# Behind the experts: joins ahead of the roots, roots in pairs, a scale that moves into the turn

## Chip, cores, metric

One core of a Trainium2 chip runs the whole network in one launch. The metric is the device time in microseconds (us). Before the change three runs gave 2161.83, 2163.40 and 2168.58 us, median 2163.4. TensorE (PE) multiplies, VectorE (DVE), ScalarE (ACT) and GpSimd (POOL) work on rows, SyncE (SP) issues the weight loads. The granted clock of TensorE has two levels, 1.2 and 2.4 GHz, shown as 0.50 and 1.00.

## What is computed

Two layers of a mixer with attention and a routed mixture of 32 experts (first block), then a dilated attention and a state-space layer (second block). The model is 1024 wide, 256 tokens in two tiles of 128, and 256 context tokens in two further tiles for layer 0. Two places of it matter here:

```
# end of layer 0: the experts' two rows per token are added, weighted; then layer 1 begins
x = x + w0 * y0 + w1 * y1
h = modulate(rmsnorm(x, norm_mix_g[1]), shift, scale)     # 4 tiles: latent and context
q, k, v = h @ odd_w_in[0]

# end of layer 1: the same sum, the final norm, and the second block's first norm
x = rmsnorm(x + w0 * y0 + w1 * y1, final_g)
h = rms_norm(x, attn_pre_norm_2[0])
h = dilated_attention_mixer(h, attn_w_in_2[0], ...)
```

## The kernel before

Each engine runs its own program, written out by hand; they meet at semaphores. `ev(name)` raises one when an instruction ends, `at(name)` is the value to wait for, `dm(name)` is raised by a DMA. `vstep` lets VectorE wait for its own last instruction. `XS[:, t, :]` holds the rows of tile t, `HT` the turned (transposed) activations, `ST` small columns of statistics, `AR` a large workspace cut by hand, `RG` the ring of weight slots, `PS[0..7]` the PSUM banks.

**Behind the experts of layer 0** (odd_begin). `act_combine` (L1934 to L1937) has ScalarE's queue load the experts' rows, one load of 1 MB for each of four tiles, `z_load0..3`. `dve_join` (L1929 to L1932) adds them to XS in two passes. ScalarE squares and sums the tile (L2005). Then the root: `dve_rstd` (L486) writes the mean (L491), ScalarE takes the square root (`act_root`, L508), VectorE inverts it and refines it with one Newton step (L493 to L501, with n=1 three tensor_scalar, with n>1 the forms with two tensors). The identity scaled by the result is `DG` (L2032), and TensorE multiplies each 128x128 block of XS by it (L1995), which scales and turns at once. ScalarE copies six of the eight blocks out of PSUM with scale and shift from `COLS` (L2017), VectorE two (L2043). `COLS` of layer 1 come from `pe_odd_cols`, `dve_odd_raw` and `dve_odd_cols` (L473, L413, L420, L423), which TensorE and VectorE do on the way. Both engines' loops are staggered over six steps: step i joins tile i, takes the root of tile i-1, copies out tile i-2. Banks alternate between tiles, so tile t waits for the copies of tile t-2.

Then `pe_odd` projects (L2074 for the first weights). In between it turns the bias of the attention (L2110), 7 heads at a time. `act_odd` loads what that needs from ScalarE's queue: it waits until tile 3 is turned, issues three table loads (L2115, L2117) and then the bias loads (L2096). SP issues the weights of layer 1 (L3134) once `z_load3` has landed (L3116).

**Behind the experts of layer 1** (final, L2324 to L2358). Two tiles. VectorE joins both, multiplying each by final_g (`gained`, L2341); ScalarE squares the rows before and after that (L2325, L2328). Then, tile after tile on VectorE: the root of the final norm, its square into the sum of the gained rows (L2346, L2348), the root of the next norm, the product of both (L2350), and the rows multiplied by that and by attn_pre_norm_2, `PG1` (L2351, into `W1[t]`). `pe_turn` transposes W1[t] against the plain identity (L533), ScalarE copies the halves into HT (L539), and L2501 is the first projection of the dilated attention. The scaled rows themselves go back into XS (L2354). POOL has no part; its next work is the masks (L2660), behind `mask_load` and `finished`. ScalarE's exponential and sine (L2362 to L2368) and VectorE's tables (L2384 on) run beside the first projections.

Of the kernel before, what the change touches and what calls it, by code (L numbers as in the profile page):

```python
# [155 lines left out]
def build(nc, I, K, out, stop=None, dump=None):  # L156
    ctx = ExitStack()
    with ctx:
# [1821 lines left out]
        DG = [ar(0, 128), ar(KK, 128)]  # L1980
# [5 lines left out]
        def pe_odd_begin(pe):  # L1986
            pe_odd_cols(pe)
            for t in range(4):
# [4 lines left out]
                for k in range(8):  # L1993
                    bank, c = odd_bank_of(t, k)
                    m = pe.matmul(bank[:, c:c + 128], XS[:, t, 128 * k:128 * k + 128], DG[t % 2], start=True, stop=True,  # L1995
                                  skip_group_check=True)
                    if k in (5, 7):
                        m.then_inc(*ev("turned", "mix1", t, k // 7))

        def act_odd_begin(act):  # L2000
            act.dma_start(AB[:, 4:12], I["ada_b_pad"][1][:, 4:12]).then_inc(*dm("ab2_load"))
            for i in range(6):
                if i < 4:
                    act.wait_ge(*at("joined_rows", i))
                    act.activation(E0.Z[i][:, 0, :], XS[:, i, :], ACT.Square,  # L2005
                                   accum_out=ST[:, i:i + 1]).then_inc(*ev("squares", ("mix1", i)))
                if 1 <= i <= 4:
                    t = i - 1
                    act_root(act, ("mix1", t), at_=t)
                if i >= 2:  # L2010
                    t = i - 2
                    if t == 0:
                        act.wait_ge(*at("ada_cols", 1, 3))
                    act.wait_ge(*at("turned", "mix1", t, 0))
                    for k in range(6):
                        bank, c = odd_bank_of(t, k)
                        ins = act.activation(HT[:, k, 128 * t:128 * t + 128], bank[:, c:c + 128],  # L2017
                                             ACT.Identity, scale=COLS[1][:, 1, t // 2, k:k + 1],
                                             bias=COLS[1][:, 0, t // 2, k:k + 1])
                    ins.then_inc(*ev("turned_out", "mix1", t, 0))  # L2020

        def dve_odd_begin(v):
            for i in range(6):
                if i < 4:
                    v.wait_ge(*at(f"z_load{i}", 0))
                    dve_join(v, E0, i, ev("joined_rows", i))
                if 1 <= i <= 4:
                    t = i - 1
                    dve_rstd(v, ("mix1", t), D, at_=t)
                    if t >= 2:  # L2030
                        v.wait_ge(*at("turned", "mix1", t - 2, 1))
                    v.tensor_scalar(DG[t % 2], IDN[:], ST[:, 16 + t:17 + t], None, MUL).then_inc(*ev("diagonal", t))  # L2032
                if i == 1:
                    dve_odd_raw(v, 1)
                if i == 2:
                    dve_odd_cols(v)
                    v.wait_ge(*at("ada_cols", 1, 3))
                if i >= 2:
                    t = i - 2
                    v.wait_ge(*at("turned", "mix1", t, 1))  # L2040
                    for k in range(6, 8):
                        bank, c = odd_bank_of(t, k)
                        ins = v.tensor_scalar(HT[:, k, 128 * t:128 * t + 128], bank[:, c:c + 128],  # L2043
                                              COLS[1][:, 1, t // 2, k:k + 1], COLS[1][:, 0, t // 2, k:k + 1], MUL, ADD)
                    ins.then_inc(*ev("turned_dve", "mix1", t, 1))
# [275 lines left out]

        def act_final(act):
            for t in range(2):
# [6 lines left out]
                act_root(act, ("final", t), at_=t)  # L2330
                act_root(act, ("dil", t), at_=2 + t)
# [906 lines left out]
```

## Time and profile before

| | |
|---|---|
| median of 3 runs | 2163.4 us |
| profiled execution, its own time | 2162.5 us |
| its span | 2160.7 us |
| PE busy | 1963.8 us (91%) |
| DVE busy | 657.7 us (30%) |
| ACT busy | 371.1 us (17%) |
| POOL busy | 321.8 us (15%) |
| DMA, mean | 269 GB/s |

In a timeline a row is: start, time covered, engine, line, operation, out<-in, how many instructions were merged; in brackets the idle time of the engine before them and what ended it. A suffix q is the engine's queue, here the issue of DMAs; PEld loads weights. Two records stand for one matmul in float32. A transpose has one record.

### The profile page before, as it was taken

How to read it: one execution, taken by the hardware profiler on the slowest of the kernel's cores; microseconds unless marked ns; L12 is line 12 of the kernel's file. 1: busy time of each engine (PE TensorE's matmuls, PEld its weight loads, DVE VectorE, ACT ScalarE, POOL GpSimd, SP SyncE). 2: the span in 40 equal slices, each digit the busy share in tenths (PEclk: the TensorE clock that was granted, in tenths of full speed). 3: DMA queues.
4: the chain of work that ended last, by engine and by line, in shares of the span. 5: the costliest groups of instructions: out<-in, count | busy, mean ns of one | idle time of the engine just before them, and what ended most of it. 6: DMA issues, size and time to landing. Idle time of an engine off the chain costs nothing.

```text
span 2160.7 us, 33840 instructions
## 1 busy us (share of the span) xinstructions
PE 1963.8 (91%) x14657; PEld 1221.4 (57%) x14657; DVE 657.7 (30%) x1544; ACT 371.1 (17%) x825; POOL 321.8 (15%) x264
## 2 busy tenths in 40 slices
PE   5999999999999859999999989988859999997998
PEld 3565565555555445546555444444346676674884
DVE  1334373212222232115331111111145031145752
ACT  3133410000000020113310000000021220132131
POOL 0125411000000000114310000000020060040120
PEclk9999999999999979999999999999979999998999
DMA  9352399999999985217399999999764314417221
GB/s 366 130 199 97 120 381 408 426 427 427 426 425 426 425 325 157 84 43 274 129 381 426 427 423 427 426 421 426 334 243 156 140 57 156 143 53 195 79 90 59
DMA packets 129617, 581.14 MB, mean 269 GB/s; under 512 B 19178, under 2 KB 30602, under 8 KB 104752
## 3 DMA queue, kind: packets, MB, share of 16 engines
q1 hardware_dynamic: 103856, 545.28, 63.3%
q10 hardware_dynamic: 19488, 27.16, 3.7%
q0 software_dynamic: 6112, 6.39, 0.8%
q8 instruction: 121, 1.98, 0.4%
q14 instruction: 40, 0.33, 0.0%
HBM read 569.21 MB, written 21.38 MB: 273 GB/s over the span
## 4 chain that ended last, share of the span: by engine, by line
PE 68%; DMA 19%; DVE 6%; issue 3%; ACT 2%; POOL 2%; ACTq 1%; SPq 0%; POOLq 0%; DVEq 0%
DMA RG<-in_moe_w 16%; PE banks L1524 13%; PE banks L2501 8%; PE banks L1549 6%; PE banks L1500 4%; PE banks L2503 4%; PE banks L1076 4%; PE banks L2074 3%; PE banks L667 3%; PE banks L2076 3%; PE banks L2702 3%; PE banks L2899 2%; PE banks L797 2%; PE banks L341 2%; PE banks L825 2%
## 5 line engine op out<-in xcount | busy, mean ns | idle before, releaser
L1524 PE MATMUL banks<-RG,HT 128*64 128x256 f32 x3616 | 429.1, 391 | 31.9 <-DMA RG<-in_moe_w 29.8
L1524 PEld LDWEIGHTS banks<-RG,HT 128*64 128x64 f32 x3616 | 252.3, 135 | 215.1 <-DMA RG<-in_moe_w 48.3
L1754 POOL DMA_INDIRECT y_rows<-AR x64 | 64.0, 1000 | 871.1 <-DVE AR L1563 870.5
L1533 DVE TENSOR_TENSOR AR<-AR,banks 128x256 f32<-128x256 f32 x64 | 38.6, 603 | 481.4 <-ACT AR L1529 430.3
L1549 PE MATMUL banks<-RG,AR 128*64 128x512 f32 x752 | 171.7, 598 | 3.6 <-DVE AR L1542 3.1
L2501 PE MATMUL banks<-HT,RG 128*128 128x256 f32 x768 | 170.2, 383 | 0.7 <-ACT HT L539 0.7
L2501 PEld LDWEIGHTS banks<-HT,RG 128*128 128x128 f32 x768 | 147.0, 192 | 23.4 <-issue 2.4
L1529 ACT ACTIVATE AR<-banks 128x256 f32<-128x256 f32 x64 | 24.5, 383 | 747.2 <-PE banks L1524 747.2
L1500 PE MATMUL banks<-AR 128*128 128x256 bf16 (+1 forms) x1152 | 149.4, 277 | 2.0 <-DVE AR L1488 1.5
L1500 PEld LDWEIGHTS banks<-AR 128*128 128x128 bf16 x1152 | 108.5, 98 | 33.6 <-issue 18.3
L1549 PEld LDWEIGHTS banks<-RG,AR 128*64 128x64 f32 x752 | 50.0, 136 | 94.2 <-issue 83.4
L2074 PE MATMUL banks<-HT,RG 128*128 128x256 f32 (+1 forms) x256 | 87.4, 500 | 3.8 <-ACT HT L2017 1.8
L2503 PE MATMUL banks<-RG,HT 128*128 128x512 f32 x192 | 84.1, 594 | 0.0
L1076 PE MATMUL banks<-RG,HT 128*128 128x512 f32 x192 | 83.3, 594 | 0.8 <-DVE HT L887 0.8
L341 PE MATMUL banks<-RG,SC 128*32 128x128 f32 x1536 | 55.5, 306 | 28.9 <-DMA RG<-in_ada_w 18.2
L904 POOL TENSOR_SCALAR AR<-AR,ST 128x768 f32<-128x768 f32 (+1 forms) x24 | 45.0, 1883 | 245.6 <-DVE ST L882 245.2
L904 POOL TENSOR_SCALAR AR<-AR,SVT 128x512 f32<-128x512 f32 x27 | 42.0, 1563 | 216.8 <-DVE SVT L882 216.7
L2074 PEld LDWEIGHTS banks<-HT,RG 128*128 128x128 f32 x256 | 49.4, 196 | 42.0 <-issue 36.3
L667 PE MATMUL banks<-RG,HT 128*128 128x512 f32 (+1 forms) x192 | 69.0, 521 | 1.7 <-DVE HT L647 1.7
L341 PEld LDWEIGHTS banks<-RG,SC 128*32 128x32 f32 x1536 | 48.5, 124 | 35.5 <-issue 29.1
L1513 ACT ACTIVATE HT<-banks 128x256 f32<-128x256 f32 x128 | 49.0, 383 | 104.7 <-PE banks L1500 104.7
L1549 PE MATMUL banks<-AR 128*64 128x512 f32 x272 | 62.1, 598 | 1.0 <-DVE AR L1542 1.0
(473 smaller groups left out, 2402.4 us busy)
## 6 DMA issues: line engine op xcount, KB each, us to landing
RG<-in_moe_w SPq DMA_DIRECT2D x160, 2048.0 KB, 24.1
AR<-in_moe_w SPq DMA_DIRECT2D x32, 2048.0 KB, 12.2
RG<-in_ada_w SPq DMA_DIRECT2D x24, 2048.0 KB, 8.4
RG<-in_attn_w_in SPq DMA_DIRECT2D x20, 2048.0 KB, 7.6
RG<-in_odd_w_in SPq DMA_DIRECT2D x6, 2048.0 KB, 25.7
RG<-in_ssm_w_in SPq DMA_DIRECT2D x4, 2048.0 KB, 9.5
AR<-y_rows ACTq DMA_DIRECT2D x6, 1024.0 KB, 7.0
RG<-in_even_w_in SPq DMA_DIRECT2D x2, 2048.0 KB
```

Source lines behind the costliest of these rows:

```text
L341: m = pe.matmul(q[32 * j:32 * j + 32, :], SC[:, k, :], w[:, k, 128 * j:128 * j + 128], start=k == 0, stop=k == 7, skip_group_check=True)
L667: m = pe.matmul(PS[b][:, 0:wd], HT[:, k, 128 * t:128 * t + 128], w[:, k, :], start=k == 0, stop=k == 7)
L904: g.tensor_scalar(u["pb"][x], u["pb"][x], A.small_of(s, 3)[:, x:x + 1], None, MUL).then_inc(*ev("weighed_pool", name, s, x))
L1076: m = pe.matmul(PS[b], HT[:, k, 128 * t:128 * t + 128], w[:, k, :], start=k == 0, stop=k == 7)
L1500: m = pe.matmul(p, E.HB[t][:, i, k, :], E.one_hot(g, t), start=t == 0 and i == 0, stop=t == E.nt - 1 and i == 2)
L1524: m = pe.matmul(p[64 * h:64 * h + 64, 256 * i:256 * i + 256], x[:, k, :], w[:, h, k], start=k == 0, stop=k == 7, skip_group_check=True)
L1549: m = pe.matmul(q[64 * h:64 * h + 64, :], x, w2[:, i, 512 * h:512 * h + 512], start=i == 0, stop=i == 3)
L2074: m = pe.matmul(p[:, 0:wd], w[:, k, 128 * j:128 * j + 128], HT[:, k, 0:wd], start=k == 0, stop=k == 7)
L2076: m = pe.matmul(p, HT[:, k, 128 * j:128 * j + 128], w[:, k, :], start=k == 0, stop=k == 7)
L2501: m = pe.matmul(p[:, 0:256], w[:, k, 128 * j:128 * j + 128], HT[:, k, 0:256], start=k == 0, stop=k == 7)
L2503: m = pe.matmul(p, HT[:, k, 128 * j:128 * j + 128], w[:, k, :], start=k == 0, stop=k == 7)
L2702: m = pe.matmul(PS[2 * h + t], src[:, k, 128 * t:128 * t + 128], w[:, k, :], start=k == 0, stop=k == 7)
```

## The change

In the first place all four joins stand ahead of the later work: VectorE joins tiles 0, 1 and 2 (with the modulation steps of layer 1 between), takes the root of tile 0, joins tile 3, takes the root of tile 1, and then the roots of tiles 2 and 3 in one pass of two columns. Copies out of PSUM come behind all that. There are four diagonals instead of two, so none waits for another's use. Of tiles 2 and 3 VectorE copies four blocks out, ScalarE four. A one-element square root ahead of ScalarE's first square loads the table of roots.

In the second place the roots of both tiles are taken together, again with an early one-element root. W1[t] is the gained row times PG1, without the scale; VectorE makes W1[0], POOL makes W1[1]. The scale goes into two diagonals, `DG2`, and TensorE multiplies by them instead of transposing.

```diff
-        DG = [ar(0, 128), ar(KK, 128)]
+        DG = [ar(128 * t, 128) for t in range(4)]
+
+        def odd_on_act(t):
+            return 6 if t < 2 else 4
...
-                    m = pe.matmul(bank[:, c:c + 128], XS[:, t, 128 * k:128 * k + 128], DG[t % 2], start=True, stop=True,
+                    m = pe.matmul(bank[:, c:c + 128], XS[:, t, 128 * k:128 * k + 128], DG[t], start=True, stop=True,
                                   skip_group_check=True)
-                    if k in (5, 7):
+                    if k in (odd_on_act(t) - 1, 7):
...
         def act_odd_begin(act):
+            act.activation(ST[:, 62:63], IDN[:, 0:1], ACT.Sqrt)
+            for i in range(4):
+                act.wait_ge(*at("joined_rows", i))
+                act.activation(E0.Z[i][:, 0, :], XS[:, i, :], ACT.Square,
+                               accum_out=ST[:, i:i + 1]).then_inc(*ev("squares", ("mix1", i)))
+                if i in (1, 2):
+                    act_root(act, ("mix1", i - 1), at_=i - 1)
+            act_root(act, ("mix1", 3), n=2, at_=2)
+            act.wait_ge(*at("ada_cols", 1, 3))
+            for t in range(4):
+                act.wait_ge(*at("turned", "mix1", t, 0))
+                for k in range(odd_on_act(t)):
...
+        def dve_odd_begin(v):
+            for i in range(4):
+                v.wait_ge(*at(f"z_load{i}", 0))
+                dve_join(v, E0, i, ev("joined_rows", i))
+                if i == 0:
+                    dve_odd_raw(v, 1)
+                if i == 1:
+                    dve_odd_cols(v)
+                if i >= 2:
+                    dve_rstd(v, ("mix1", i - 2), D, at_=i - 2)
+                    dve_diagonal(v, i - 2)
+            v.wait_ge(*at("squares", ("mix1", 2)))
+            dve_rstd(v, ("mix1", 3), D, n=2, at_=2)
+            for t in (2, 3):
+                dve_diagonal(v, t)
+            v.wait_ge(*at("ada_cols", 1, 3))
+            for t in range(4):
+                v.wait_ge(*at("turned", "mix1", t, 1))
+                for k in range(odd_on_act(t), 8):
...
+        DG2 = [ar(KK + 128 * t, 128) for t in range(2)]
+
         def act_final(act):
+            act.activation(ST[:, 63:64], IDN[:, 0:1], ACT.Sqrt)
...
-                act_root(act, ("final", t), at_=t)
-                act_root(act, ("dil", t), at_=2 + t)
+            act_root(act, ("final", 1), n=2, at_=0)
+            act_root(act, ("dil", 1), n=2, at_=2)
...
+            v.wait_ge(*at("gained", 0))
+            v.tensor_tensor(W1[0], AF[0], PG1, MUL).then_inc(*ev("normed", "dil", 0))
+            first, second, s2, w = ST[:, 16:18], ST[:, 18:20], ST[:, 2:4], ST[:, 52:54]
+            dve_rstd(v, ("final", 1), D, n=2)
+            vstep(v, v.tensor_tensor(w, first, first, MUL))
+            v.wait_ge(*at("squares", ("dil", 1)))
+            vstep(v, v.tensor_tensor(s2, s2, w, MUL))
+            dve_rstd(v, ("dil", 1), D, n=2, at_=2, summed=True)
+            vstep(v, v.tensor_tensor(w, first, second, MUL))
             for t in range(2):
-                v.scalar_tensor_tensor(out=W1[t], in0=AF[t], scalar=w, in1=PG1, op0=MUL, op1=MUL).then_inc(
-                    *ev("normed", "dil", t))
+                v.tensor_scalar(DG2[t], IDN[:], w[:, t:t + 1], None, MUL).then_inc(*ev("diagonal", "dil", t))
...
+        def pool_final(g):
+            g.wait_ge(*at("final_loads", 1))
+            g.wait_ge(*at("gained", 1))
+            g.tensor_tensor(W1[1], AF[1], PG1, MUL).then_inc(*ev("dil_gained"))
+
         def pe_final(pe):
             for t in range(2):
-                pe_turn(pe, "dil", t, W1[t], ("normed", "dil", t), None)
+                pe.wait_ge(*at("diagonal", "dil", t))
+                if t == 1:
+                    pe.wait_ge(*at("dil_gained"))
+                for k in range(8):
+                    m = pe.matmul(PS[4 + 2 * t + k // 4][:, 128 * (k % 4):128 * (k % 4) + 128], W1[t][:, 128 * k:128 * k + 128],
+                                  DG2[t], start=True, stop=True, skip_group_check=True)
+                    if k % 4 == 3:
+                        m.then_inc(*ev("turned", "dil", t, k // 4))
```

## Rows read from the trace of the kernel before

**Rows 1.** The page, part 4: the chain that ended last, by line.
```profile
DMA RG<-in_moe_w 16%; PE banks L1524 13%; PE banks L2501 8%; PE banks L1549 6%; PE banks L1500 4%; PE banks L2503 4%; PE banks L1076 4%; PE banks L2074 3%; PE banks L667 3%; PE banks L2076 3%; PE banks L2702 3%; PE banks L2899 2%; PE banks L797 2%; PE banks L341 2%; PE banks L825 2%
```

**Rows 2.** Timeline, 755 to 812 us: joins, roots, turns of the first stretch.
```profile
778.49 1.28 DVE L1931 SCALAR_TENSOR_TENSOR XS<-AR,XS 128x1024 f32<-128x1024 f32 x1 [11.01 <-DMA AR<-y_rows]
...
788.86 3.62 PE L1995 MATMUL banks<-AR,XS 128*128 128x128 f32 x16
...
793.01 2.13 PE L1995 MATMUL banks<-AR,XS 128*128 128x128 f32 x16 [0.53 <-DVE AR L2032]
...
793.28 2.20 ACT L2017 ACTIVATE HT<-banks,SVT 128x128 f32<-128x128 f32 x6 [1.60 <-DVE SVT L423]
...
799.62 0.14 DVE L491 TENSOR_SCALAR ST<-ST 128x1 f32<-128x1 f32 x1
...
800.98 0.29 DVE L2032 TENSOR_SCALAR AR<-IDN,ST 128x128 f32<-128x128 f32 x1
...
804.62 0.55 ACTq L2115 DMA_DIRECT2D AR<-in_k_rev  x1
804.62 0.73 DVE L2043 TENSOR_SCALAR HT<-banks,SVT 128x128 f32<-128x128 f32 x2 [1.76 <-PE banks L1995]
```

**Rows 3.** Timeline, 803 to 905 us: first projection, bias loads, bias turn.
```profile
806.43 15.77 PE L2074 MATMUL banks<-HT,RG 128*128 128x256 f32 x64 [1.85 <-ACT HT L2017]
806.49 11.69 ACTq L2096 DMA_DIRECT2D AR<-in_na_bias  x7
...
822.47 5.69 PE L2110 MATMUL banks<-AR 64*128 64x448 f32 x14 [0.27 <-DMA AR<-in_na_bias]
```

**Rows 4.** Chain of waits in order of time, 740 to 830 us: start, us, what.
```profile
784.81 1.28 ACT L508
...
816.80 5.62 DMA AR<-in_na_bias
```

**Rows 5.** Timeline, 1563 to 1612 us: gain, scalar chain of tile 0, last transposes.
```profile
1581.15 1.22 DVE L2341 TENSOR_TENSOR AR<-XS,AR 128x1024 f32<-128x1024 f32 x1
1582.29 0.15 DVE L491 TENSOR_SCALAR ST<-ST 128x1 f32<-128x1 f32 x1
...
1585.41 0.16 DVE L2350 TENSOR_TENSOR ST<-ST 128x1 f32<-128x1 f32 x1
...
1591.46 1.97 PE L533 MATMUL banks<-IDN,AR 128*128 128x128 f32 x8 [2.48 <-DVE AR L2351]
```

**Rows 6.** Timeline, 1594 to 1760 us: projections, POOL's masks, VectorE's first table products.
```profile
1594.12 30.16 PE L2501 MATMUL banks<-HT,RG 128*128 128x256 f32 x128 [0.69 <-ACT HT L539]
...
1600.00 14.17 POOL L2660 TENSOR_TENSOR AR<-AR 128x768 f32<-128x768 f32 x8 [32.07 <-DMA AR<-in_k_dm]
...
1612.54 1.68 DVE L2384 TENSOR_TENSOR SVT<-SVT 128x32 f32<-128x32 f32 x1 [19.80 <-ACT SVT L2362]
1614.14 0.18 DVE L2385 TENSOR_TENSOR SVT<-SVT 128x32 f32<-128x32 f32 x1
...
1637.85 27.79 PE L2501 MATMUL banks<-HT,RG 128*128 128x256 f32 x128
```

**Rows 7.** Waits of SP's queue, 740 to 1100: total us, times, longest.
```profile
SPq L3134 <- PE banks L2074: 108.3, 4, 33.2
```

**Rows 8.** Experts' rows: issues (tile view, 765 to 800), landing; weights' issues (timeline).
```profile
L1936 ACTq DMA_DIRECT2D AR<-y_rows x4: 377/492/783, 773.3 to 775.0; - x4
...
DMA to landing us min/median/max: 5.1/8.7/12.0
...
787.06 15.32 SPq L3134 DMA_DIRECT2D RG<-in_odd_w_in  x5
```

**Rows 9.** Windows: busy of PE, PEld, DVE, ACT, POOL; granted clock, DMA share, GB/s.
```profile
807.00:808.00 1.00, 1.00 (x4) 0.75 (x3) 0.00 (x0) 0.00 (x0) 0.00 (x0) 0.50 1.05 387
```

**Rows 10.** Groups on POOL by form: busy us, mean ns, idle before.
```profile
L563 POOL TENSOR_TENSOR AR<-AR 128x1024 f32<-128x1024 f32 x1 | 2.3, 2345 | 1.5 <-DVE AR L550 1.5
```

**Rows 11.** Windows, the microsecond in which the clock rises behind the second stretch.
```profile
1598.00:1599.00 1.00, 1.00 (x4) 0.79 (x4) 0.00 (x0) 0.00 (x0) 0.00 (x0) 0.63 0.91 329
```

More of the change, by code:

```diff
@@ L2001, in act_odd_begin @@
             act.dma_start(AB[:, 4:12], I["ada_b_pad"][1][:, 4:12]).then_inc(*dm("ab2_load"))
[L2002 to L2009, printed above, removed]
-                if i >= 2:
[L2011 to L2045, printed above, removed]
@@ new lines, in act_odd_begin @@
+            for t in range(4):
+                act.wait_ge(*at("turned", "mix1", t, 0))
+                for k in range(odd_on_act(t)):
+                    bank, c = odd_bank_of(t, k)
+                    ins = act.activation(HT[:, k, 128 * t:128 * t + 128], bank[:, c:c + 128],
+                                         ACT.Identity, scale=COLS[1][:, 1, t // 2, k:k + 1],
+                                         bias=COLS[1][:, 0, t // 2, k:k + 1])
+                ins.then_inc(*ev("turned_out", "mix1", t, 0))
@@ new lines, in dve_diagonal @@
+        def dve_diagonal(v, t):
+            v.tensor_scalar(DG[t], IDN[:], ST[:, 16 + t:17 + t], None, MUL).then_inc(*ev("diagonal", t))
+        def dve_odd_begin(v):
[6 more added lines that the diff above has]
+                    dve_odd_cols(v)
+                if i >= 2:
+                    dve_rstd(v, ("mix1", i - 2), D, at_=i - 2)
[8 more added lines that the diff above has]
+                for k in range(odd_on_act(t), 8):
+                    bank, c = odd_bank_of(t, k)
+                    ins = v.tensor_scalar(HT[:, k, 128 * t:128 * t + 128], bank[:, c:c + 128],
+                                          COLS[1][:, 1, t // 2, k:k + 1], COLS[1][:, 0, t // 2, k:k + 1], MUL, ADD)
+                ins.then_inc(*ev("turned_dve", "mix1", t, 1))
@@ L2341, in dve_final @@
                 v.tensor_tensor(AF[t], XS[:, t, :], FG, MUL).then_inc(*ev("gained", t))
-            for t in range(2):
-                first, second = ST[:, 16 + t:17 + t], ST[:, 18 + t:19 + t]
-                s2, w = ST[:, 2 + t:3 + t], ST[:, 52 + t:53 + t]
-                dve_rstd(v, ("final", t), D, at_=t)
-                vstep(v, v.tensor_tensor(w, first, first, MUL))
-                v.wait_ge(*at("squares", ("dil", t)))
-                vstep(v, v.tensor_tensor(s2, s2, w, MUL))
-                dve_rstd(v, ("dil", t), D, at_=2 + t, summed=True)
-                vstep(v, v.tensor_tensor(w, first, second, MUL))
-                v.scalar_tensor_tensor(out=W1[t], in0=AF[t], scalar=w, in1=PG1, op0=MUL, op1=MUL).then_inc(
-                    *ev("normed", "dil", t))
+            v.wait_ge(*at("gained", 0))
```

1 line of the change is left out of this document (added).

## Prediction

> **What bounds the kernel now.** I read the page's chain first, to see which work ends last: TensorE and the expert weights hold most of it, and neither of the two places that the change touches has a line of its own there [rows 1]. So the prize is bounded by two short stretches without matmuls, one behind the first set of experts and one behind the second. For these I read the timeline.
>
> In the first stretch (778 to 806 us) VectorE joins a tile (two passes of 1.28 us), takes its root, turns to the next. TensorE turns tile 2 and 3 as soon as each diagonal is there, and starts the projection L2074 at 806.43 [rows 2, 3]. What follows is decided by a second runner: the seven bias loads, issued by ScalarE's queue from 806.49. The last lands at 822.42 (816.80 and 5.62), when TensorE has just finished its 64 matmuls and waits 0.27 us for it [rows 3, 4]. The two are tied; a gain needs both to come earlier.
>
> In the second stretch (1574 to 1594 us) VectorE is the only busy engine: joins, gains, then two scalar chains one behind the other, each with a pass of 1.28 us over the rows. The last transposes start at 1591.46, L2501 at 1594.12 [rows 5, 6].
>
> Is a gain here kept? The queue that issues the weights waits for TensorE, not for the time [rows 7], so what comes later moves along. I count a microsecond as a microsecond.
>
> **Part 1, tiles joined ahead.** The four row loads are issued between 773.3 and 775.0 and land after 5.1 to 12.0 us, the last at 787.0; the third at about 784 if they are spaced evenly (an estimate) [rows 8]. After the change VectorE has: join 0 to 781.1, the small modulation steps and join 1 to about 784.2, join 2 to 787.0, the root of tile 0 with its diagonal. That chain costs 1.65 us: 799.62 to 800.98, and 0.29 for the diagonal [rows 2]. So diagonal 0 at 788.7, join 3 to 791.2 (its data lies there since 787.0), diagonal 1 at 792.9, then one chain for tiles 2 and 3: diagonals at 794.5 and 794.7. Before, the last one stood at 801.27. Three chains stand where four stood, and nothing on TensorE's side comes between. The changed waits: VectorE's copies out of PSUM are queued behind all joins, and so are ScalarE's, which start at 793.1 instead of 793.3; TensorE waits with tile 2 for both.
>
> TensorE: tile 0, turned behind a standstill, costs 3.62 us and tile 1 2.13 [rows 2]; I read the two as the low and the full clock. Tile 0 from 788.7 to 792.3; tile 1 from 792.9; tile 2 when ScalarE has copied tile 0 out (793.1 and 2.20), at 795.4; tiles 2 and 3 at the full clock to 799.8. Then VectorE's four copies of tile 3, 2 x 0.73, so **L2074 starts at about 801.3, 5.1 us earlier**. If the clock falls between, tiles 2 and 3 take 3.62 each, and it is 804.2, 2.2 earlier. I take the first: TensorE has now hardly a gap of over 1 us from 788.7 on, where before it stood idle from 795.1 until diagonal 2 came.
>
> Copies moved from ScalarE to VectorE (two for each of tiles 2 and 3): 4 x 0.37 = 1.5 us less on ScalarE, the same more on VectorE, in parallel with it; it is in the sum. The table load of 1.28 us goes to about 776, where ScalarE waits for the join; it lay ahead of root 0 alone, and that root is no longer on the path (join 3 is). It is worth nothing by itself here. I weigh the two new one-element activations at 0.2 us each, hidden there; were the cover gone, 1.5 us on the path.
>
> **Bias loads.** The queue comes to them when tile 3 is turned: first the table issues at 804.62, the first bias issue 1.87 us later at 806.49 [rows 2, 4]. Now that is 799.8 and 801.7, 4.8 us earlier. Their landing moves by 4.8 at most. At least by 0: if the weight loads issued from 787.06 on (five of 2 MB, 15.3 us of issues [rows 8]) hold the DMA engines, the small loads only wait longer. Seven took 11.69 us to issue in that traffic. I take 819.0, 3.4 us earlier, being nearer to the end that the issue times set.
>
> TensorE itself would be done earlier: 128 such matmuls take 27.79 us at the full clock [rows 6], so 64 take 13.9, and 801.3 plus 13.9 is 815.2. The 1.9 us that the cold stretch in L2074 costs now (15.77 against 13.9, granted clock 0.50 at 807 [rows 9]) go as well, but under the bias. So TensorE **waits almost 4 us for the bias**, a new wait. What that does: a standstill of 1.85 us ahead of 806.43 was followed by a stretch at 0.50 [rows 3, 9]. I take the same price again behind the new wait, 1.9 us; between 0 and 2.4 (30.16 against 27.79 in the colder start [rows 6]). First stretch: -3.4 + 1.9 = **-1.5 us**, between -4.8 and +2.4.
>
> **Part 2, the end.** Two scalar chains and two passes of 1.28 become one pass, one chain and two diagonals. From 1582.29, when the last gain is done: W1[0] is multiplied by the gain, 1.23, to 1583.5. The chain from mean to weight was 3.28 (1582.29 to 1585.57 [rows 5]): 1586.8. Diagonal, 0.29: 1587.1. The squares of tile 1 run on ScalarE beside W1[0], a pass of about the same length, and are hidden; the table load was no longer on the path, and isn't now.
>
> POOL is new here: it makes W1[1], 2.35 us by the nearest row of its size (L563 [rows 10]), from the same event that lets VectorE start W1[0]. Here the trace warns. At 1612.54 a VectorE product of 128x32 took 1.68 us, its neighbour of the same size 0.18; it ended at 1614.22, just when POOL's run of eight products ended at 1614.17 [rows 6]. So a product of two SBUF tensors on VectorE stands still until POOL's is over. VectorE is first with W1[0]; POOL starts at 1583.5, ends at 1585.9; the chain's first product, due at 1584.2, waits till then: **+1.7 us**, the diagonal at 1588.8. Bounds: 0 if they don't meet, 2.35 if POOL is first. The Trainium skill, SBUF — State Buffer, section Who interferes with whom, says that a VectorE instruction with two SBUF inputs and a GpSimd instruction that reads SBUF exclude each other for the whole instruction, whoever issues first; by that rule the delay is there, and the row agrees. Without it the sum below would be about 1.2 better.
>
> TensorE: the turn is now a true matmul against the diagonal: 3.62 cold or 2.13, where a transpose run took 1.97 cold [rows 2, 5]. That is a cost of 1.65 for each cold tile, but TensorE then works without a pause from 1588.8. Now the clock rises only at 1598.7, 0.63 in that microsecond [rows 11], because TensorE stood still for 2.48 us ahead of 1591.46 [rows 5]. I take the rise at about 1592: tile 0 to 1592.4, tile 1 to 1594.5, last copy 0.7 (1593.43 to 1594.12 now): **L2501 at 1595.2**. That is 1.1 later than 1594.12, but with the full clock, which gives back 30.16 - 27.79 = 2.4: **-1.3 us**. Bounds: -2.5 without POOL's lock (start 1594.0), +2.6 when both tiles and the start of L2501 stay cold.
>
> The scaling of the result rows moves behind the diagonals and nobody waits for it: POOL's masks wait for a load that ScalarE's queue issues after the turn. SP's loads hang on the row loads, as before.
>
> **Sum.** -1.5 - 1.3 = -2.8 us. The profiled execution took 2162.5, its span 2160.7; the sum gives 2159.7. The median of the runs is 0.9 above the profiled one: **2160.6 us**, 0.13% less. A difference of under 0.3% (6.5 us) can't be told from none here.
>
> **Rivals.**
> (a) *No cold stretch behind the bias, no meeting with POOL.* For it: the bias may land before the clock reacts, and VectorE's chain has few products of two tensors. Then -4.8 and -2.5: 2162.5 - 7.3 + 0.9 = **2156.1**, faster by 0.34%. Against: the row at 1612.54, and the weights under way [rows 8]. Chance 0.17.
> (b) *The bias doesn't move, TensorE cools.* The loads stay behind the weights and land at 822.4 or later; TensorE stands still 7 us from 815.2, starts at half speed, and the early start of L2074 brings only a longer wait: 0 + 2.4 - 1.3 = +1.1, **2164.5**, slower than before, if the bias lands later than about 820. For it: the DMA engines are full until then. Against: the bias loads are small and have a queue of their own. Chance 0.15.
> (c) *Cold tiles.* Tiles 2 and 3 are turned at the low clock, L2074 starts at 804.2 and the bias issues 1.9 earlier; TensorE and bias stay tied, no new wait: -1.9 - 1.3, **2160.2**. The time alone won't tell it from mine. Chance 0.13.
> (d) *The early load does nothing*: the table is loaded again at the first root. It costs 1.3 us at a place that isn't on the path: no change to the sum. Chance 0.03.
> (e) *The end loses*: both turned tiles and L2501's start stay cold, stage two +2.6: -1.5 + 2.6 = +1.1, 2164.5. Chance 0.07.
> Mine has 0.45.
>
> **Numbers.** Range 2154.5 to 2165.5: from below (a) to above (b) and (e), with a margin of 1 to 1.5 us on each side, since runs of one kernel lie further apart than that. Faster by over 0.3% is most of (a): 0.15. Slower by over 0.3% needs (b) and (e) together and more: 0.04. Within: 0.81.
>
> **What would show it.** First stretch: four joins with no DMA wait after the third, L508 once for tiles 2 and 3, L2074 near 801, and TensorE idle ahead of L2110 until in_na_bias, about 4 us, followed by slices at 0.50. Second: W1[0] at 1.23, then a product on VectorE of over 1 us that ends with POOL's; turned tiles of 16 records, the second faster; L2501's 128 matmuls in about 28 instead of 30.16. Wrong if L2110 waits under 1 us, if the bias lands before 818, or if no product on VectorE is stretched; also if the expert stream behind either stretch takes longer than before by what was gained.

## The result, and the profile after

The changed kernel took 2175.8 us (median of 7 runs, 2171.39 to 2178.39), the kernel before on the same chip 2163.97 (7 runs): ratio 1.0042, 95% interval 1.0024 to 1.0059. It is **slower by 0.42%**, some 9 us (5 to 13 by the interval), where 2.8 us less were forecast; the medians lie 11.8 apart. The span of the one profiled execution of each kernel grew by 13.6 us, from 2160.7 to 2174.3. A second measurement (run e13_after below) gave 1.0038 (1.0025 to 1.005).

The head of the page after:

```profile
span 2174.3 us, 33855 instructions
PE 1967.1 (90%) x14673; PEld 1222.7 (56%) x14673; DVE 657.4 (30%) x1531; ACT 370.0 (17%) x820; POOL 324.8 (15%) x265
```

The first stretch in the timeline of after, 755 to 815 us. Here and below, matmuls are counted as records, two for each, as the prediction counts them; only the 14 that e6_fill adds are counted as the code does (x28 in the view). Lines have moved: the projection is L2078 (was L2074), the turn of the bias L2114 (L2110), the bias loads L2100 (L2096), SP's weights L3155 (L3134), the turn of the rows L1999 (L1995).

```profile
786.89 28.23 SPq L3155 DMA_DIRECT2D RG<-in_odd_w_in  x6
788.51 3.78 PE L1999 MATMUL banks<-AR,XS 128*128 128x128 f32 x16 [6.72 <-DVE AR L2025]
792.59 6.57 PE L1999 MATMUL banks<-AR,XS 128*128 128x128 f32 x48 [0.30 <-DVE AR L2025]
...
800.67 14.05 PE L2078 MATMUL banks<-HT,RG 128*128 128x256 f32 x64 [1.51 <-ACT HT L2019]
801.06 13.91 ACTq L2100 DMA_DIRECT2D AR<-in_na_bias  x7
```

So far everything went as forecast: the projection starts at 800.67 (801.3 was forecast, 806.43 it was [rows 3]), takes 14.05 instead of 15.77, and the bias loads go out at 801.06 (801.7 forecast, 806.49 before). One thing is easily missed: SP's row counts six issues, all out by 815.12. Before, five were out by 802.38 [rows 8] and the sixth came only at 822.23. TensorE's rows in the next stretch, 795 to 880 us of after:

```profile
828.31 10.82 PE L2114 MATMUL banks<-AR 64*128 64x448 f32 x14 [13.59 <-DMA AR<-in_na_bias]
839.06 30.36 PE L2078 MATMUL banks<-HT,RG 128*128 128x512 f32 x64
869.35 5.62 PE L2114 MATMUL banks<-AR 64*128 64x448 f32 x14
```

and the same of before, where they follow the turn at 822.47 [rows 3]:

```profile
828.09 27.73 PE L2074 MATMUL banks<-HT,RG 128*128 128x512 f32 x64
855.75 5.62 PE L2110 MATMUL banks<-AR 64*128 64x448 f32 x14
```

**Here lies the whole loss.** The second turn of the bias starts at 869.35 against 855.75: 13.6 us later, which is all that the span of these two executions grew by. In three terms: the last bias load lets TensorE go at 828.31 instead of 822.47, +5.8; the 14 matmuls that turn the bias take 10.8 instead of 5.7, +5.1; the 64 behind them 30.3 instead of 27.7, +2.6. TensorE stands idle for 13.59 us where it stood for 0.27.

The times of these stages are compared from now on as "stage": from the first issue of layer 1's weights (787.06 before, 786.89 after), which falls with the landing of the experts' rows, to the second turn of the bias. Before: 68.7. After: 82.5.

**Why the bias came late.** SP issues the sixth weight load when TensorE has read the first one and so freed its slot of the ring (SP's queue waits for that [rows 7]). SP's issues in the timeline of after (807 to 830), then of before (806 to 824):

```profile
814.75 0.37 SPq L3155 DMA_DIRECT2D RG<-in_odd_w_in  x1
```

```profile
822.23 0.37 SPq L3134 DMA_DIRECT2D RG<-in_odd_w_in  x1
```

Before, the sixth load went out when the bias was nearly through. TensorE, now 7.5 us earlier at the end of its first 64 matmuls, sends it 2 MB into the traffic that the bias loads are still in. The DMA view shows what that does. Its columns: queue, packets, MB, share of 16 engines; q1 is SP's queue, q10 ScalarE's. Before, 810 to 814 us:

```profile
q1 hardware_dynamic: 522, 1.04, 80.8%
q10 hardware_dynamic: 519, 0.24, 25.0%
```

before, 814 to 819:

```profile
q1 hardware_dynamic: 665, 1.33, 78.5%
q10 hardware_dynamic: 1283, 0.32, 32.1%
```

before, 819 to 822.4, with the weights gone:

```profile
q10 hardware_dynamic: 1550, 0.38, 76.1%
```

and after, 815 to 822:

```profile
q1 hardware_dynamic: 1062, 2.14, 89.9%
q10 hardware_dynamic: 1063, 0.26, 17.9%
```

While both queues have work they advance **packet for packet**: 522 and 519 in before, 1062 and 1063 in after, and between 822 and 826 us of after 605 and 605. A packet of the weights is 2 KB, one of the bias 256 bytes. So beside weights the bias gets 152 packets per us (1063 in 7), and alone it got 456 (1550 in 3.4). The seven loads of 112 KB are 3136 packets; half of them went through in the last 3.4 us of before. A further weight load is 1024 packets, 6.7 us at 152 per us, and in those the bias stays at the slow rate; alone, as many packets of it would need 2.2 us. So the load costs the bias some 4.5 us by these rates (an estimate; 5.5 was measured, see e3_hold). The Trainium skill, DMA: Bandwidth & Descriptors, section Queues, rings and completion order, says that each DMA engine serves the queues that have work in turn, a packet at a time; the equal counts agree. The page gives a packet as some 9 to 17 descriptors, and the profile counts single pieces of 256 bytes or 2 KB, so the counts show equal turns and not how long one turn is.

**Why TensorE was slow behind it.** Windows of after: TensorE's busy time is the first entry, then PEld, DVE, ACT, POOL; behind them the granted clock, the DMA share and GB/s.

```profile
815.00:819.00 4.00, 0.00 (x0) 0.00 (x0) 0.00 (x0) 1.21 (x4) 0.00 (x0) 0.76 1.08 344
819.00:822.00 3.00, 0.00 (x0) 0.00 (x0) 0.00 (x0) 0.00 (x0) 0.00 (x0) 0.50 1.08 343
...
828.30:834.00 5.70, 5.69 (x8) 2.80 (x9) 3.01 (x6) 0.00 (x0) 0.00 (x0) 0.50 0.19 25
...
839.00:845.00 6.00, 6.00 (x9) 2.59 (x9) 1.11 (x2) 0.00 (x0) 0.00 (x0) 0.55 0.33 48
845.00:850.00 5.00, 5.00 (x13) 2.15 (x12) 0.00 (x0) 0.60 (x1) 0.00 (x0) 1.00 0.00 0
```

The clock falls to 0.50 (1.2 GHz) in the standstill and stays there through all of the bias matmuls, although TensorE is busy without a gap from 828.3 (10.82 us, against 5.69 in before at a granted clock of 1.00); it is back at 1.00 only in the projection that follows. Before, the stretch at 0.50 behind the short standstill [rows 9] had only a price of 1.7 (15.77 against 14.05).

**The second stretch** went nearly as forecast. Timeline of after, 1578 to 1640 us (L2351 and L2367 make W1[0] and W1[1], L491 the mean, L2360 the diagonals, L2375 the turn, L2521 the projection that was L2501):

```profile
1597.43 1.22 DVE L2351 TENSOR_TENSOR AR<-AR 128x1024 f32<-128x1024 f32 x1
...
1597.69 3.15 POOL L2367 TENSOR_TENSOR AR<-AR 128x1024 f32<-128x1024 f32 x1 [14.86 <-DVE AR L2349]
...
1598.56 2.30 DVE L491 TENSOR_SCALAR ST<-ST 128x2 f32<-128x2 f32 x1
...
1601.34 0.16 DVE L499 TENSOR_TENSOR ST<-ST 128x2 f32<-128x2 f32 x1
...
1604.17 6.09 PE L2375 MATMUL banks<-AR 128*128 128x128 f32 x32 [23.22 <-DVE AR L2360]
...
1610.95 27.89 PE L2521 MATMUL banks<-HT,RG 128*128 128x256 f32 x128 [0.69 <-ACT HT L539]
```

From the first join (1589.87 after, 1574.73 before) to L2521 it is 21.08 us, where it was 19.39; but L2521's 128 matmuls take 27.89 instead of 30.16 [rows 6]. The product on VectorE that POOL should hold up is there, 0.16 us long and unharmed: what stood still is the mean, a tensor_scalar of two columns, 2.30 us.

### The profile page after: what moved, and what is told of

Read it like the earlier page. It is cut to its first block, busy times and chain, and to the rows that moved or that the text cites. A ratio compares the mean times of both kernels' runs of the same rounds, so it can differ in the third digit from the quotient of the medians.

```text
span 2174.3 us, 33855 instructions
## 1 busy us (share of the span) xinstructions
PE 1967.1 (90%) x14673; PEld 1222.7 (56%) x14673; DVE 657.4 (30%) x1531; ACT 370.0 (17%) x820; POOL 324.8 (15%) x265
## 4 chain that ended last, share of the span: by engine, by line
PE 67%; DMA 20%; DVE 5%; ACT 2%; issue 2%; POOL 2%; ACTq 1%; SPq 0%; POOLq 0%; DVEq 0%
DMA RG<-in_moe_w 17%; PE banks L1524 13%; PE banks L2521 8%; PE banks L1549 6%; PE banks L2523 4%; PE banks L1076 4%; PE banks L1500 4%; PE banks L2078 3%; PE banks L667 3%; PE banks L2080 3%; PE banks L2722 3%; PE banks L2919 2%; POOL AR L904 2%; PE banks L341 2%; PE banks L797 2%
## 5 line engine op out<-in xcount | busy, mean ns | idle before, releaser
L2521 PE MATMUL banks<-HT,RG 128*128 128x256 f32 x768 | 168.0, 380 | 0.7 <-ACT HT L539 0.7
L2521 PEld LDWEIGHTS banks<-HT,RG 128*128 128x128 f32 x768 | 145.4, 190 | 22.6 <-issue 2.4
L2078 PE MATMUL banks<-HT,RG 128*128 128x256 f32 (+1 forms) x256 | 88.3, 503 | 3.4 <-ACT HT L2019 1.5
L2078 PEld LDWEIGHTS banks<-HT,RG 128*128 128x128 f32 x256 | 49.2, 196 | 43.4 <-issue 38.6
```

The source lines that it names most:

```text
L2078: m = pe.matmul(p[:, 0:wd], w[:, k, 128 * j:128 * j + 128], HT[:, k, 0:wd], start=k == 0, stop=k == 7)
L2521: m = pe.matmul(p[:, 0:256], w[:, k, 128 * j:128 * j + 128], HT[:, k, 0:256], start=k == 0, stop=k == 7)
```

## The experiments

Two theories stood at first. **T1, the backlog:** the bias lands when the DMA engines have worked off what was issued before and beside it; the early slot adds 2 MB, the standstill takes the clock. **T2, the issue:** the bias follows its own issue, and something else in part 1 costs the time (T2 is the prediction's own step). A third for the size: **T3, the clock alone** makes most of it. All ratios below are against the kernel before on the same chip, with the 95% interval. The weights' first issue shifts from trace to trace by up to 4.6 us with the experts ahead; the stage leaves that out. What lies outside the stage varies too, with no order by the edits: from the stage's end to the first join of the second stretch it is 719.0 us in before and 720.2 to 722.7 in the thirteen others, and from 1945 us or so to the end 209.4 to 213.1. So a span of one execution is good to some 3 us, and the ratios to what their intervals say.

**e1_joins: part 1 alone**, the end as before.

```diff
         def act_final(act):
-            act.activation(ST[:, 63:64], IDN[:, 0:1], ACT.Sqrt)
...
-            act_root(act, ("final", 1), n=2, at_=0)
-            act_root(act, ("dil", 1), n=2, at_=2)
+                act_root(act, ("final", t), at_=t)
+                act_root(act, ("dil", t), at_=2 + t)
...
```

> The change behind the first experts alone, the end as before. Theory A (the whole loss sits there: the bias loads land later, 828 instead of 822 us, because TensorE frees a weight slot earlier and the sixth 2 MB load joins the traffic, and TensorE cools while it waits): about 13 to 15 us slower than before, 2177 to 2179, with L2114 waiting 13 us for in_na_bias. Theory B (the loss is spread, or comes from the expert stream): less than 8 us slower.

Measured: 1.0051 (1.0035 to 1.0067), some 11 us, under the 13 to 15 expected and over the rival's 8. TensorE waits 14.2 us for the bias, the stage is 82.8.

**e2_end: part 2 alone**, the first stretch as before.

```diff
-            for t in range(2):
-                first, second = ST[:, 16 + t:17 + t], ST[:, 18 + t:19 + t]
...
+            first, second, s2, w = ST[:, 16:18], ST[:, 18:20], ST[:, 2:4], ST[:, 52:54]
+            dve_rstd(v, ("final", 1), D, n=2)
...
```

> The change at the end alone, the first place as before. Theory A: 1 to 2 us faster than before, 2162 to 2163. Theory B (POOL's product and the two-pass matmuls cost more than they give): 1 us or more slower.

Measured: 0.9986 (0.9965 to 1.0007), no change that can be told, so it doesn't decide between its two theories; its stage is 70.6, within 2 us of before. The two parts add up: 1.0051 times 0.9986 is 1.0037. The loss is part 1's.

**e3_hold: the sixth load held back** until the last bias load has landed.

```diff
+                if key == ("odd", 2, 1):
+                    sp.wait_ge(*at("bias_loads", 6))
```

> The whole change, but SP holds the sixth weight load (odd, 2, 1) until the seventh bias load has landed. Theory A (the sixth load delays the bias): the bias lands at about 820 instead of 828, TensorE waits 5 instead of 13.6 us; 8 to 12 us faster than the changed kernel, 2164 to 2168. Theory B (the five earlier weight loads alone hold the bias up): bias at 828 as before the edit, same time as the changed kernel, 2176.

Rows of the timeline of e3_hold, TensorE's and the issues of SP and ScalarE:

```profile
790.41 36.27 SPq L3157 DMA_DIRECT2D RG<-in_odd_w_in  x6
...
804.22 14.05 PE L2078 MATMUL banks<-HT,RG 128*128 128x256 f32 x64 [1.51 <-ACT HT L2019]
...
804.61 13.79 ACTq L2100 DMA_DIRECT2D AR<-in_na_bias  x7
...
826.30 10.82 PE L2114 MATMUL banks<-AR 64*128 64x448 f32 x14 [8.03 <-DMA AR<-in_na_bias]
...
837.05 29.44 PE L2078 MATMUL banks<-HT,RG 128*128 128x512 f32 x64
```

Measured: 1.001 (0.9998 to 1.0022), some 7 us faster than the changed kernel by the ratios, where 8 to 12 were expected: the wait fell to 8.0 us and not to 5. This run decides most. The bias lands 35.9 us after the first weight issue (826.30 - 790.41), against 41.4 in after (828.31 - 786.89): the sixth load costs 5.5 us. In the five traces with the early sixth load it is 41.4 to 42.0. (Landings are taken here as the start of the turn that waits for them.) And it lands 35.4 after it in the kernel before (822.47 - 787.06), **although its issue began 19.4 us after the weights' there and 14.2 here**. Five microseconds of earlier issue did not bring the landing forward: T2 falls. The DMA view from 823 to 826.3 shows the tail again:

```profile
q10 hardware_dynamic: 1162, 0.29, 53.7%
q1 hardware_dynamic: 44, 0.07, 6.6%
```

What the standstill leaves is the clock: 8.03 us of waiting still make the bias matmuls 10.82 long. The stage is 76.0, 7.3 over before; 0.5 from the landing, 6.8 from the clock (5.1 and 1.7).

**e6_fill: the standstill filled** with 14 matmuls whose result nobody reads, after the first projection.

```diff
+                if c == 0:
+                    for x in range(14):
+                        pe.matmul(PS[4], HT[:, x % 8, 0:128], HT[:, x % 8, :], start=True, stop=True)
```

> The whole change, plus 14 matmuls of 128x512 into a free bank between the first projection and the bias turn: 12.1 us of work without a use, inside a wait of 13.6 us. Theory A (over half of the loss is TensorE's clock after that wait: the 14 bias matmuls took 10.8 instead of 5.7 us, the next 64 30.3 instead of 27.7): the granted clock stays at 1.00, 7 us faster than the changed kernel, about 2168.5. Theory B (the slow matmuls come from the DMA traffic or from VectorE): no faster, 2176.

The timeline of e6_fill on TensorE:

```profile
816.41 12.18 PE L2110 MATMUL banks<-HT 128*128 128x512 f32 x28
...
830.44 8.94 PE L2117 MATMUL banks<-AR 64*128 64x448 f32 x14 [1.84 <-DMA AR<-in_na_bias]
...
839.31 29.36 PE L2078 MATMUL banks<-HT,RG 128*128 128x512 f32 x64
```

and one of its windows, columns as above:

```profile
832.80:836.00 3.20, 3.20 (x5) 1.34 (x4) 3.10 (x6) 0.00 (x0) 0.00 (x0) 0.50 0.53 82
```

Measured: 1.0005 (0.999 to 1.0019), the 7 us that were expected, but not in the way that was expected. The bias lands as late as in after, 41.7 us after the weights. The clock is up when its matmuls begin, but is down from 832.8 on, in the midst of them, behind a wait of only 1.84 us. Of the 7.7 us that the clock costs in after, 4.9 remain here (8.94 - 5.69 and 29.36 - 27.73). The stage is 79.9, 2.6 less than after; the profiled span is 4.1 less, the ratio by about 0.35% (some 7 us) better. The stage explains only a part of that ratio; the rest is open. Where the clock is down the bias matmuls are slow, here too, so T3 has its part; but the late landing alone is 5.8 of the 13.6 us, and T3 is not the whole.

**e5_short: the mirror, on the kernel before.** It leaves half of the first projection's products out (k 3 to 6 of 8 on the first weight), so TensorE frees the slot early; no other line is changed.

```diff
-            for k in range(8):
+            for k in ((0, 1, 2, 7) if c == 0 and hf == 0 else range(8)):
```

> The kernel before, where the first projection of layer 1 leaves out half of its matmuls (k 3 to 6 of 8), 7 us of TensorE's work less; nothing else is changed, so the bias loads are issued when they were. Theory A (ending that projection early hands a slot to the sixth weight load, which delays the bias by 6 us, and TensorE cools): 12 to 14 us slower than before though it does less. Theory B (the sixth load is innocent): the bias lands where it did, 35.4 us after the first weight issue; 0 to 8 us slower by the clock alone.

Timeline of e5_short, weights from 791.26:

```profile
812.00 8.86 PE L2074 MATMUL banks<-HT,RG 128*128 128x256 f32 x32 [1.85 <-ACT HT L2017]
...
833.30 10.82 PE L2110 MATMUL banks<-AR 64*128 64x448 f32 x14 [12.44 <-DMA AR<-in_na_bias]
```

Measured: 1.0037 (1.0018 to 1.0057), stage 81.9. By the time alone, some 8 us, this lies between its theories (12 to 14, and up to 8); the landing decides. **A kernel that does less is as slow as the changed one.** No join, root or diagonal has moved here; the sixth load goes out at 820.9, 29.6 us after the first instead of 35.2, and the bias lands at 42.0, as in after, where it was 35.4. (Its issue, too, began 1.4 us later than before, 20.8 after the weights; by e3_hold that moves nothing.) That shows the mechanism without the change.

**e4_early: six of the seven bias loads on ScalarE's queue at the very start**, behind the loads of the rows.

```diff
+            for h in range(6):
+                act_bias_load(act, h)
...
-            for h in range(7):
+            for h in range(6, 7):
```

> The whole change, and six of the first seven bias loads are issued at the start of the stage, behind the row loads on the same queue and ahead of the weights; one stays where it was. Theory A (the wait ahead of the bias turn is the whole loss): that wait goes to under 1 us, the bias matmuls take 5.7 us again, the stage from the first weight issue to the second bias turn takes 61 us (82.5 in the changed kernel, 68.7 before): 21 us faster than the changed kernel, 9 to 10 us faster than before (ratio 0.9955). Rival B (the one load that is left, with the tables, lands as late as seven do, since the weights hold it up): the wait stays over 8 us, less than 7 us gained on the changed kernel.

ScalarE in the timeline of e4_early, and then TensorE's turn of the bias there:

```profile
780.58 10.35 ACTq L2102 DMA_DIRECT2D AR<-in_na_bias  x4
...
790.98 1.06 ACT L2011 ACTIVATE AR<-XS 128x1024 f32<-128x1024 f32 x1 [10.78 <-DVE XS L1932]
```

```profile
820.72 5.69 PE L2116 MATMUL banks<-AR 64*128 64x448 f32 x14
```

Measured: 0.9963 (0.9949 to 0.9977), some 8 us faster than before (9 to 10 expected), stage 64.4. There is no wait for the bias and no cold stretch. But issues occupy the engine's program: ScalarE's first square stands 10.78 us, its own queue being in the way, and the projection starts 17.1 us after the weights instead of 13.8. The stage was expected at 61; those 3.3 us are what is missing.

**e8_best: e4_early, and VectorE makes both W1**, so that POOL has no part.

```diff
+            v.wait_ge(*at("gained", 1))
+            v.tensor_tensor(W1[1], AF[1], PG1, MUL).then_inc(*ev("normed", "dil", 1))
...
-            g.tensor_tensor(W1[1], AF[1], PG1, MUL).then_inc(*ev("dil_gained"))
...
```

> As e4_early, and at the end VectorE makes both gained rows, POOL none. Theory A: 1 us of the 2.2 that the first mean stands still behind POOL comes back net of VectorE's own pass of 1.2: the end stage (first join to first projection) takes 20.1 instead of 21.1 us; 10 to 11 us faster than before (ratio 0.995). Theory B: no difference to e4_early, since the pass and the standstill cost the same.

Timeline of e8_best on VectorE:

```profile
1582.52 1.22 DVE L2355 TENSOR_TENSOR AR<-AR 128x1024 f32<-128x1024 f32 x1
1583.66 0.16 DVE L491 TENSOR_SCALAR ST<-ST 128x2 f32<-128x2 f32 x1
```

Measured: 0.9956 (0.9942 to 0.9971). The mean takes 0.16 instead of 2.30, at the price of a pass of 1.22. From join to diagonals 12.86 us, 13.86 in after; to the projection 20.50 (20.1 expected), 21.08 in after. Half a microsecond won; against e4_early the times don't tell it.

**e10_before_early: the same six loads, on the kernel before.**

```diff
+            for h in range(6):
+                act_bias_load(act, h)
...
```

> The kernel before with only the six bias loads issued early, the joins, roots and turns as they were. Theory A (bias and first projection were tied before, so freeing one of them gives nothing): 0 to 1 us from before. Rival: the bias traffic slowed something else in the stage (weights, rows), and moving it gives over 3 us by itself.

Measured: 1.0007 (0.9994 to 1.002), stage 71.3. The bias is there in time, but nothing waited for it before either (0.27 us), and ScalarE's standstill moves the projection to 24.0 us after the weights, from 19.4. On this queue the early bias is worth something only with the joins ahead, and these only with the bias out of their way.

**e11_spbias: the six loads on SP's queue, ahead of the first weight**, on after without POOL's product.

```diff
                 if key == ("odd", 0, 0):
                     sp.wait_ge(*at("z_load3", 0))
+                    for h in range(6):
+                        src6 = bass.AP(I["na_bias"].tensor, h * 465 + 76, [[1, 64], [31, 7], [1, 64]])
+                        sp.dma_start(SG[h][0:64].rearrange("p (a b) -> p a b", a=7), src6).then_inc(*dm("bias_first", h))
...
```

> The changed kernel with VectorE making both gained rows at the end, and six of the first seven bias loads issued by SP's queue, behind the last row load and ahead of the first weight, so that ScalarE's squares don't stand behind their issue (in e4_early they stood 10.8 us). Theory A: the first projection starts 14 to 17 us after the row loads have landed (13.8 in the changed kernel, 17.1 in e4_early), no wait ahead of the bias turn, the stage 2 to 3 us shorter than in e4_early; 12 to 13 us faster than before (ratio 0.9942). Rival: the weights land later by the bias traffic and TensorE waits for the first of them: no better than e8_best (0.9956).

Timeline of e11_spbias on TensorE:

```profile
805.82 15.74 PE L2078 MATMUL banks<-HT,RG 128*128 128x256 f32 x64 [4.43 <-DMA RG<-in_odd_w_in]
```

Measured: 0.9955 (0.9941 to 0.9969), where 0.9942 was expected: its rival is what came, no better than e8_best. No engine stands behind the issues, but the weights go out 4.1 us late, and TensorE waits 4.43 us for the first one instead. The stage, from 788.54 on, is 66.2.

**e12_before_spbias: the same on the kernel before.**

```diff
+                    for h in range(6):
+                        src6 = bass.AP(I["na_bias"].tensor, h * 465 + 76, [[1, 64], [31, 7], [1, 64]])
+                        sp.dma_start(SG[h][0:64].rearrange("p (a b) -> p a b", a=7), src6).then_inc(*dm("bias_first", h))
...
```

> The kernel before with six bias loads issued by SP's queue as in e11, nothing else. Theory A (joins and turns set the start of the first projection, the bias only ties with its end): within 1 us of before. Rival: the bias loads were in the way of something, over 3 us faster.

Measured: 0.9976 (0.9964 to 0.9988), stage 68.4 against 68.7. Within 1 us was expected; the times are 0.24% lower, some 5 us, clear of noise, which is the rival's size. The two profiled executions don't place it: the stage is 0.3 us shorter, and from the second stretch's first join to the projections near 1945 us it is 371.40 against 373.09, but between them 2.4 longer. Open.

**e13_after: the changed kernel once more**, on the chip of e11 and e12.

> The changed kernel again, on the chip of the others: 0.4 to 0.5% slower than before, as measured first (1.0042); bias wait of TensorE 13 to 14 us.

Measured: 1.0038 (1.0025 to 1.005); TensorE waits 13.4 us for the bias. The result stands a second time.

**e14_spmid: as e11, but the bias loads behind the first weight load**, which is needed first.

```diff
                 if key == ("odd", 0, 0):
                     sp.wait_ge(*at("z_load3", 0))
+                if key == ("odd", 1, 0):
+                    for h in range(6):
+                        src6 = bass.AP(I["na_bias"].tensor, h * 465 + 76, [[1, 64], [31, 7], [1, 64]])
+                        sp.dma_start(SG[h][0:64].rearrange("p (a b) -> p a b", a=7), src6).then_inc(*dm("bias_first", h))
...
```

> As e11_spbias, but the six bias loads are issued behind the first weight load instead of ahead of it. In e11 TensorE waited 4.4 us for that first weight. Theory A: the first projection starts 13.8 us after the row loads have landed, as in the changed kernel, no wait ahead of the bias turn, the stage (row loads landed to second bias turn) 61 to 62 us against 68.7 before and 82.5 in the changed kernel; 12 to 13 us faster than before (ratio 0.9942). Rival: the bias loads, now behind 2 MB of weights, land after the first projection's end and TensorE waits and cools again: slower than e11 (0.9955).

Timeline of e14_spmid, SP's queue and TensorE:

```profile
790.56 0.37 SPq L3160 DMA_DIRECT2D RG<-in_odd_w_in  x1
790.97 8.04 SPq L3142 DMA_DIRECT2D AR<-in_na_bias  x6
...
804.59 14.05 PE L2078 MATMUL banks<-HT,RG 128*128 128x256 f32 x64 [1.51 <-ACT HT L2019]
...
818.58 5.69 PE L2115 MATMUL banks<-AR 64*128 64x448 f32 x14
...
824.20 27.73 PE L2078 MATMUL banks<-HT,RG 128*128 128x512 f32 x64
```

Measured: **0.9937** (0.9915 to 0.9959), 2156.35 us against 2169.47, the lowest ratio of all, though its interval overlaps those of e4, e8 and e11. TensorE goes from the first projection into the bias and on without a wait; the stage is 61.3, 7.4 less than before. That is what the joins ahead bring to this stretch once the bias is out of their way: 5.3 us of earlier start, 1.7 us of cold clock, and the small wait. The whole ratio is some 13.7 us, more than the stage and the second stretch (some 2) give. Against e12, which has the bias on SP's queue without the joins, it is 0.9961 (0.9937 by 0.9976, from different chips), some 8 us, and that the stage (7.1) accounts for. The other 5 are e12's, and as open as there.

## Why the prediction was wrong, point by point

**Right, first stretch up to the projection.** Start of L2078 at 801.3, measured 800.67; bias issue 801.7, measured 801.06. The tiles were turned as taken, 3.78 cold (3.62) and the rest at the full clock. Rival (c), cold tiles, falls: tiles 1, 2 and 3 take 6.57 together. The view that projection and bias are tied, and that a gain needs both, was right, and the new wait for in_na_bias is where it was put.

In short: the step that failed is the one on the bias loads. Their landing was forecast 3.4 us earlier, between 0 and 4.8, and came 5.8 us later, since the change itself starts a weight load that they have to share the DMA engines with; and the clock's price behind the wait, put at 1.9, was 7.7. These two make the 13.6 us. Against the forecast of -1.5 for the first stretch the landing is 9.2 us off (3.4 by step 1, the rest by step 2) and the clock 5.8 (step 3).

**Wrong, step 1: "Their landing moves by 4.8 at most. At least by 0 ... I take 819.0, 3.4 us earlier."** The choice between the ends fell on the wrong row. The issue times ([rows 3, 4]) looked nearest, but the landing was set by the backlog: e3_hold and before have the bias 35.9 and 35.4 us after the first weight issue, with issues 5 us apart. The trace of before had the sign of it: both queues in step from 810 to 814 us (522 and 519 packets), and half of the bias, 1550 packets, only in the 3.4 us behind the weights. Rival (b)'s mechanism was the right one here.

**Wrong, step 2: "At least by 0".** The lower end was no bound. I had written that SP's queue waits for TensorE [rows 7] and used it only to carry a gain forward. The same row says that a TensorE that finishes some 7 us early (815.2 by the forecast's own sum, 822.2 before) issues the next 2 MB some 7 us early. Nothing in the prediction asked what it would meet. Measured: 5.5 us (41.4 in after against 35.9 in e3_hold), seen once more in e5_short. By the packet counts of the kernel before it could have been worked out as an estimate: 1024 packets more at the shared rate of 130 per us (519 in 4) are 7.9 us, less 2.2 for as many packets of the bias at the 456 per us of the tail, 5.6 us.

**Wrong, step 3, the term for the clock.** "I take the same price again behind the new wait, 1.9 us; between 0 and 2.4". Measured 7.7 in after (5.1 on the bias matmuls, 2.6 on the projection), 6.8 in e3_hold. Both ends came from places where the clock came back within a few microseconds of large matmuls. Here a run of 14 matmuls on 64 rows follows the standstill, and it runs at 0.50 from end to end. Whether it is their kind or the length of the standstill that keeps the clock down, no run tells. The mechanism was named, its size was off by four.

**Rival (b)** was the nearest, at 2164.5 with a chance of 0.15: right in both its halves (the landing doesn't move, the clock is lost), short by the sixth load and by the cold bias matmuls. It is the nearest by its reasons, and still 11 us under the result. 0 + 2.4 would have had to read +5.8 + 7.7.

**Right, second stretch.** -1.3 was forecast for it. From the first join to the end of L2521's 128 matmuls it is 48.97 us after (21.08 + 27.89) and 49.55 before (19.39 + 30.16), -0.6; counted to the projections near 1945 us (373.09 before, 371.64 after) it is -1.45, and the eight experiments with the new end lie between 370.44 and 371.49. Of those with the old end three have 373.10 to 373.41, but e12_before_spbias has 371.40. That fits -1.3, though not all of it falls where it was put, and e2_end's ratio can't tell it from nothing. L2521 takes 27.89 ("about 28"); W1[0] 1.22 (1.23). POOL's delay was put at 1.7 and came to 2.15, but its victim wasn't a product of two tensors: it was the mean, which has one. The row of before that taught the rule ([rows 6]) was a product; that only products are hit didn't follow from it. The Trainium skill, SBUF — State Buffer, section Who interferes with whom, does list tensor_scalar among the operations that can, under conditions on their operands, take the shared ports; the row of 2.30 us agrees with it, and the products behind it at 0.16 come after POOL's end at 1600.84 and say nothing against it. POOL's own product took 3.15 with the wait for W1[0] in it, as the forecast had the order. Rival (e), a cold end, falls.

**"I count a microsecond as a microsecond."** Single traces can't show that to the microsecond. The stage lost 13.8, the span 13.6, because the part between the two stretches took 1.5 us longer and the second stretch gave 1.45 back; but that part takes longer than in before in every other trace, whatever the kernel, by 1.2 to 3.7, so its agreement here is partly luck. The seven runs of each kernel put the loss at 9 us (5 to 13).

**The chances.** Slower by over 0.3% had 0.04, reasoned as "needs (b) and (e) together and more". The fault was to let rivals combine only from terms that were already in the sum; none held a transfer that the change itself would start earlier.

## What to carry to other kernels

When an engine gets done earlier, ask which slot it frees, which transfer that starts and who shares the DMA engines with it; an earlier compute step can delay its own next input. Many small pieces beside large weight loads advance packet for packet and land when the large ones are through (here), so put them ahead of the traffic that isn't needed yet, on a queue whose engine has nothing else to do (e14_spmid), and not by issuing them a few microseconds sooner. And price a new wait on TensorE with the clock that it loses, over the matmuls that really follow it.

## What the runs showed of the hardware

- Two queues with work share the DMA engines by packets, not by bytes: 1062 to 1063 in 7 us, of 2 KB and of 256 bytes (522 to 519 in 4 us of before). The small ones ran at 152 packets per us beside the weights and at 456 alone.
- TensorE's granted clock stayed at 0.50 through 10.8 us of matmuls on 64 rows without a gap, and came back in the 128-row matmuls that followed (0.50 to 844, 1.00 from 845). In e6_fill it fell during them, behind 12.18 us of full work and 1.84 us of idle time.
- A tensor_scalar of 128x2 on VectorE stood 2.30 us beside a POOL product over two tensors, until that ended; without POOL it took 0.16 (e8_best). So a one-tensor instruction of the smallest size is not safe from it.
- Issues of small loads block the engine that issues them: four loads took 10.35 us of ScalarE's program in e4_early while the rows were landing; six took 8.04 on SP's queue in e14_spmid and 4.09 in e11_spbias, where no weight load went out ahead of them.
